# First loads and splits in a new order around a transposed x

## What is computed

```python
def hybrid_layer(x, mem, pos, g_mix, w_in, w_pa, w_pb, w_pm, w_o, g_mem, w_mkv, g_mlp, w_up, w_down):
    h = rms_norm(x, g_mix)
    z = h @ w_in
    ...
    o_m = memory_attn(q_m * scale, rms_norm(mem, g_mem), w_mkv)
    ...
    x = x + y @ w_o
```

## Time and profile before

| | |
|---|---|
| three runs | 1579.76, 1580.19, 1582.11 us; median 1580.19 |
| profiled execution | 1578.82 us, its span 1577.0 us |
| TensorE busy | 1429.0 us (91%) |
| VectorE, ScalarE, GpSimd busy | 576.1, 551.9, 674.3 us |
| DMA | 395.40 MB, mean 251 GB/s |
| mean granted clock of TensorE | 0.952 |

### The profile page before, as it was taken

The page is one execution under the profiler, slowest core; times in us unless marked ns, Lnnn a source line. Parts: engine busy times, 40 slices in busy tenths (PEclk is TensorE's granted clock), DMA queues, the critical chain, the costliest instruction groups (busy, mean ns, idle before and its releaser), DMA issues.

```text
span 1577.0 us, 17946 instructions
## 1 busy us (share of the span) xinstructions
PE 1429.0 (91%) x7601; PEld 1016.2 (64%) x7601; DVE 576.1 (37%) x885; ACT 551.9 (35%) x709; POOL 674.3 (43%) x187
## 2 busy tenths in 40 slices
PE   8999999999999999999999999999996676676666
PEld 7877788877887778887799888978841121121111
DVE  4522423336262242334643876768510010010001
ACT  6356443433535645444343344574310000000001
POOL 6846588755784658786655775010000000000000
PEclk9999999999999999999999999999998787787788
DMA  8534457588553445659925444013999999999997
GB/s 296 187 111 157 149 174 239 183 301 315 176 183 122 151 143 185 226 176 338 321 83 190 132 149 152 20 68 137 420 402 428 428 427 428 429 426 428 427 428 292
DMA packets 115517, 395.40 MB, mean 251 GB/s; under 512 B 5719, under 2 KB 9620, under 8 KB 101996
## 3 DMA queue, kind: packets, MB, share of 16 engines
q1 hardware_dynamic: 113372, 388.70, 66.0%
q0 software_dynamic: 1520, 4.49, 0.8%
q10 hardware_dynamic: 544, 1.05, 0.2%
HBM read 393.16 MB, written 1.05 MB: 250 GB/s over the span
## 4 chain that ended last, share of the span: by engine, by line
PE 75%; DMA 21%; ACT 1%; DVE 1%; issue 1%; SPq 1%; POOL 0%; DVEq 0%; ACTq 0%
PE psum L2282 17%; PE psum L2284 17%; PE psum L2283 17%; DMA ring<-in_w_e_down 7%; PE psum L1247 7%; DMA ring<-in_w_e_up 6%; DMA ring<-in_w_e_gate 6%; PE psum L1162 2%; PE psum L2435 1%; PE psum L2462 1%; PE psum L2326 1%; PE psum L1023 1%; PE psum L2511 1%; PE psum L821 1%; PE psum L823 1%; PE psum L822 1%
## 5 line engine op out<-in xcount | busy, mean ns | idle before, releaser
L655 POOL TENSOR_TENSOR ring_lo<-ring,ring_hi 128x2048 fp32r<-128x2048 f32 x118 | 538.7, 4572 | 230.2 <-ACT ring_hi L635 229.9
L635 ACT ACTIVATE ring_hi<-ring 128x2048 fp32r<-128x2048 f32 (+1 forms) x127 | 239.9, 1889 | 319.6 <-DMA ring<-in_w_down 104.2
L2284 PE MATMUL psum<-ring_hi,hT_hi 128*128 128x512 f32 (+2 forms) x848 | 327.8, 387 | 0.0
L2283 PE MATMUL psum<-ring_lo,hT_hi 128*128 128x512 f32 (+2 forms) x848 | 327.2, 386 | 0.0
L2282 PE MATMUL psum<-ring_hi,hT_lo 128*128 128x512 f32 (+2 forms) x816 | 323.2, 396 | 0.4 <-POOL ring_lo L655 0.2
L1247 PE MATMUL psum<-arena 128*32 128x512 f32 x796 | 141.9, 703 | 63.5 <-DMA arena<-in_w_e_down 23.4
L1247 PE MATMUL psum<-ring,arena 128*32 128x512 f32 x720 | 133.7, 732 | 61.2 <-DMA ring<-in_w_e_gate 23.6
L2284 PEld LDWEIGHTS psum<-ring_hi,hT_hi 128*128 128x128 f32 x848 | 159.3, 188 | 32.3
L2283 PEld LDWEIGHTS psum<-ring_lo,hT_hi 128*128 128x128 f32 x848 | 159.6, 188 | 28.8
L2282 PEld LDWEIGHTS psum<-ring_hi,hT_lo 128*128 128x128 f32 x816 | 153.5, 188 | 37.1 <-issue 6.1
L1247 PEld LDWEIGHTS psum<-arena 128*32 128x32 f32 x796 | 32.1, 126 | 163.3 <-issue 73.4
(11 more groups left out here) (467 smaller groups left out, 1927.8 us busy)
## 6 DMA issues: line engine op xcount, KB each, us to landing
ring<-in_w_in SPq DMA_DIRECT2D x59, 1024.0 KB, 5.1
ring<-in_w_up SPq DMA_DIRECT2D x32, 1024.0 KB, 5.5
ring<-in_w_down SPq DMA_DIRECT2D x32, 1024.0 KB, 5.6
ring<-in_w_e_down SPq DMA_DIRECT2D x16, 2048.0 KB, 20.5
arena<-in_w_e_up SPq DMA_DIRECT2D x14, 2048.0 KB, 20.4
arena<-in_w_e_down SPq DMA_DIRECT2D x12, 2048.0 KB, 23.8
ring<-in_w_e_gate SPq DMA_DIRECT2D x12, 2048.0 KB, 22.9
arena<-in_w_e_gate SPq DMA_DIRECT2D x12, 2048.0 KB, 22.8
```

What stands on the lines that cost most here:

```text
L635: act.activation(slot_hi(u)[:, 0:c, :], slot(u)[:, 0:c, :], ACT.Copy).then_inc(hi_sb, 1)
L655: eng.tensor_tensor(slot_lo(u)[:, 0:c, :], slot(u)[:, 0:c, :], slot_hi(u)[:, 0:c, :].bitcast(F32), ALU.subtract).then_inc(done, 1)
L2283: pe.matmul(dst, hi(k0 + k), w_lo, start=False, stop=False)
L2284: last = pe.matmul(dst, hi(k0 + k), w_hi, start=False, stop=stop and k == nk - 1)
```

## The change

Two new inputs are prepared: x transposed, `x_t` (features by tokens), and the gains of `norm_mix` as columns, `gain_cols`. The tile `xn`, not in use at that time, holds the transposed x as `xT`.

- **Loads.** ScalarE issues the first half of xT (512 features, rows of 1 KB). SyncE issues the gain columns ahead of the identity, then unit 0 in four pieces, unit 1 in two halves, the second half of xT, units 2 and 3, and the small rows, the `norm_mix` rows now among them. Token-major x is one load, which ScalarE issues when unit 2 has landed; memory and the constants go when unit 3 has landed.
- **TensorE.** The transposes of the gain rows and of both halves of x in layer 0 are gone. The identity is multiplied five times instead of four. Unit 1 is done in halves (`second_unit`).
- **ScalarE.** For each k: a block of `hT_hi` from `xT`, then a piece of unit 0. Then unit 1 in halves, the second half of `hT_hi`, the x load, units 2 and 3, the squares of x (their junk output in `x_sq` instead of `xn`), unit 4, and the wait for memory as before.
- **VectorE.** For each k a block of `hT_lo` and a piece of unit 0, then unit 1 in halves, the second half of `hT_lo`, and the low part of unit 2, which was GpSimd's.
- Counts of the semaphores follow.

```diff
-LO_VECTOR = [(l, u) for l in range(DEPTH) for u in SPLIT if (l == 0 and u < 2) or (u >= 50 and u % 4 == 2)]
+LO_VECTOR = [(l, u) for l in range(DEPTH) for u in SPLIT if (l == 0 and u < 3) or (u >= 50 and u % 4 == 2)]
...
         def _(sp):
             sp.sem_inc(slots_free, R1)
+            sp.dma_start(cols[:, 0:16], w["gain_cols"]).then_inc(const_in, 16)
             sp.dma_start(consts[:, 0:P], w["consts"][:, 0:P]).then_inc(const_in, 16)
...
-            gain_rows(0, "norm_mix", const_in)
...
+                    if l == 0 and u == 1:
+                        for half in range(2):
+                            cs = slice(2 * half, 2 * half + 2)
+                            sp.dma_start(slot(1)[:, cs, :], src[:, cs, :]).then_inc(landed(1) if half else half_in, 16)
+                        sp.dma_start(xT[:, 4:8, :], x_src[:, 4:8, :]).then_inc(rest_in, 16)
+                        continue
                     load(u, src, l * UNITS1 + u + 1)
                     if l == 0 and u == R1 - 1:
+                        gain_rows(0, "norm_mix", late_in)
...
             pe.wait_ge(const_in, 32)
-            pe.transpose(psum[:, 7, 0:16], rows1[0:16, :], ident[0:16, 0:16]).then_inc(cols_full, 1)
-            pe.wait_ge(x_in, 16)
-            half_to_features(x, 0)
-            keep_busy(6, 4)
+            keep_busy(6, 5)
             first_unit()
-            pe.wait_ge(rest_in, 16)
-            half_to_features(x, 1)
+            second_unit()
...
+            def second_unit():
+                for half in range(2):
+                    pe.wait_ge(lo_v, UC + half + 1)
+                    for t in range(TT):
+                        last = split_product(DB[1][:, t, :], tokens(hT_hi, t), tokens(hT_lo, t), 2 * half, 1, nk=2, first=2 * half,
+                                             start=half == 0, stop=False)
+                last.then_inc(slots_free, 1)
...
-            low_piece(0)
-            low_half(0, g_feat[:, 0, 0, :], 0)
-            for k in range(1, UC):
+            dve.wait_ge(const_in, 32)
+            for k in range(UC):
+                dve.wait_ge(turn_a, k + 1)
+                dve.scalar_tensor_tensor(out=hT_lo[:, k, :], in0=xT[:, k, :], scalar=g_feat[:, 0, 0, k:k + 1],
+                                         in1=hT_hi[:, k, :].bitcast(F32), op0=ALU.mult, op1=ALU.subtract).then_inc(turn_lo, 1)
                 low_piece(k)
-            split_lo(dve, 0, 1)
+            for half in range(2):
+                cs = slice(2 * half, 2 * half + 2)
+                dve.wait_ge(hi_sb, UC + half + 1)
+                dve.tensor_tensor(slot_lo(1)[:, cs, :], slot(1)[:, cs, :], slot_hi(1)[:, cs, :].bitcast(F32), ALU.subtract).then_inc(lo_v, 1)
...
-                low_half(1, g_feat[:, 0, l, :], l * 18 + 4)
+                low_half(1, g_feat[:, 0, l, :], l * 18 + 4, None if l else xT)
                 if l == 0:
-                    dve.wait_ge(cols_full, 2)
+                    split_lo(dve, 0, 2)
+                    dve.wait_ge(cols_full, 1)
...
-            x_src = w["x"].rearrange("b (t p) d -> p (b t) d", p=P)
-            act.dma_start(x[:, :, 0:UN], x_src[:, :, 0:UN]).then_inc(x_in, 16)
-            act.dma_start(x[:, :, UN:D], x_src[:, :, UN:D]).then_inc(rest_in, 16)
+            act.dma_start(xT[:, 0:4, :], w["x_t"].rearrange("(c p) t -> p c t", p=P)[:, 0:4, :]).then_inc(x_in, 16)
...
-            high_piece(0)
-            act.wait_ge(cols_sb, 1)
-            high_half(0, g_feat[:, 0, 0, :], 1)
-            for k in range(1, UC):
+            act.wait_ge(const_in, 32)
+            act.wait_ge(x_in, 16)
+            for k in range(UC):
+                act.activation(hT_hi[:, k, :], xT[:, k, :], ACT.Copy, scale=g_feat[:, 0, 0, k:k + 1]).then_inc(turn_a, 1)
                 high_piece(k)
+            for half in range(2):
+                cs = slice(2 * half, 2 * half + 2)
+                act.wait_ge(slot_in[1] if half else half_in, 16)
+                act.activation(slot_hi(1)[:, cs, :], slot(1)[:, cs, :], ACT.Copy).then_inc(hi_sb, 1)
+            high_half(1, g_feat[:, 0, 0, :], 0, xT)
+            act.wait_ge(slot_in[2], 16)
+            act.dma_start(x[:, :, :], w["x"].rearrange("b (t p) d -> p (b t) d", p=P)).then_inc(x_in, 16)
...
                 if l == 0:
-                    high_parts(1, 2)
+                    high_parts(2, 3)
+                    act.wait_ge(x_in, 32)
+                    squares_half(0, sums, x_sq)
+                    squares_half(1, sums, x_sq)
+                    high_parts(4, 4)
...
-            pool.wait_ge(rest_in, 16)
-            pool.wait_ge(slot_in[2], 16)
+            pool.wait_ge(slot_in[3], 16)
             pool.dma_start(mem_tok, w["mem"].rearrange("b (t p) d -> p (b t) d", p=P)).then_inc(mem_in, 16)
             pool.dma_start(consts[:, P:], w["consts"][:, P:]).then_inc(mem_in, 16)
```

More of the change, by code:

```diff
@@ L164 @@
 N_ROWS2 = sum(r[2] for r in ROWS2)
-N_LATE = 2 + len(ROWS2)
+N_LATE = 3 + len(ROWS2)
 PIECES = UC - 1
+EXTRA = PIECES + 1
 def rows_of(a):
@@ L286, in build @@
         mem_sq = carve(18688, TT, D)
+        x_sq = carve(16384, TT, D)
+        xT = xn[:, :, :].rearrange("p t (c n) -> p (t c) n", n=T)
         kv_mem = carve(14848, TT, 2 * WM)
@@ L2569, in _, with low_half @@
         def _(dve):
-            def low_half(half, gain, ready):
+            def low_half(half, gain, ready, features=None):
                 for k in range(4):
@@ L2574, in low_half @@
                         dve.wait_ge(turn_a, ready + k + 2)
-                    dve.scalar_tensor_tensor(out=hT_lo[:, 4 * half + k, :], in0=flat[2 + half][:, k * T:(k + 1) * T],
+                    src = flat[2 + half][:, k * T:(k + 1) * T] if features is None else features[:, 4 * half + k, :]
+                    dve.scalar_tensor_tensor(out=hT_lo[:, 4 * half + k, :], in0=src,
                                              scalar=gain[:, 4 * half + k:4 * half + k + 1],
@@ L2679, in _ @@
                 for half in range(2):
-                    dve.wait_ge(turn_full, l * 8 + 3 + half)
+                    dve.wait_ge(turn_full, l * 8 + 1 + half)
                     for k in range(4):
@@ L2888, in _, with high_half, squares_half @@
         def _(act):
[L2889 to L2890 removed]
+            def high_half(half, gain, full, features=None):
+                if features is None:
+                    act.wait_ge(turn_full, full)
+                else:
+                    act.wait_ge(rest_in, 16)
                 for k in range(4):
[L2892 removed]
+                    src = flat[2 + half][:, k * T:(k + 1) * T] if features is None else features[:, 4 * half + k, :]
+                    act.activation(hT_hi[:, 4 * half + k, :], src, ACT.Copy,
                                    scale=gain[:, 4 * half + k:4 * half + k + 1]).then_inc(turn_a, 1)
[L2895 removed]
+            def squares_half(half, into, junk=xn):
                 for t in range(TT):
[L2897 removed]
+                    act.activation(junk[:, t, half * UN:(half + 1) * UN], x[:, t, half * UN:(half + 1) * UN], ACT.Square, accum_out=into[:, t, half:half + 1])\
                        .then_inc(sq_a, 1)
[L2900 to L2902 removed]
+            act.dma_start(xT[:, 0:4, :], w["x_t"].rearrange("(c p) t -> p c t", p=P)[:, 0:4, :]).then_inc(x_in, 16)
             act.wait_ge(cleared, 1)
@@ L2990, in high_y @@
                 def high_y(half):
-                    act.wait_ge(turn_full, l * 8 + 5 + half)
+                    act.wait_ge(turn_full, l * 8 + 3 + half)
                     act.activation(hT_hi[:, 4 * half:4 * half + 4, :], flat[2 + half].rearrange("p (k t) -> p k t", k=4), ACT.Copy,
@@ L3063 @@
     arrays["consts"] = constants()[1]
+    arrays["x_t"] = np.ascontiguousarray(np.asarray(inputs["x"])[0].T)
+    arrays["gain_cols"] = np.ascontiguousarray(np.asarray(inputs["norm_mix"]).reshape(16, P).T)
     nc = bacc.Bacc("TRN2", target_bir_lowering=False, num_devices=1, dynamic_dma_scratch_size=8192)
```

48 lines of the change are left out of this document (19 added, 29 removed).

## The result

| | before | after |
|---|---|---|
| median of 21 runs each | 1580.79 us | 1582.91 us |
| ratio after / before | | 1.0018, 95% from 1.0012 to 1.0023 |
| profiled execution, its span | 1578.82, 1577.0 us | 1582.06, 1580.3 us |
| start of unit 0, 1, 2, 3 on TensorE | 9.10, 16.26, 22.17, 27.75 | 7.96, 15.06, 20.87, 26.44 |
| start of unit 4 on TensorE | 34.85 | 37.88 |

The change makes the kernel slower by 0.18%, 2.9 us, with an interval of 1.9 to 3.6 us; the difference of the two medians is 2.1 us and lies inside it. One of the 21 runs before took 2928.48 us, and the ratio leaves it out. The forecast was no change. TensorE leads by 1.1 to 1.3 us as far as unit 3 and is 3.0 us behind from unit 4 on.

What follows compares the result with a forecast made beforehand. Bound: TensorE's progress before about 1100 us, which moves the expert-weight tail. Unit 4: TensorE alone 34.85 - 2.1 = 32.8, z's tile 28.7 + 6.1 = 34.8; the later counts, so no change: 1580.2 us, range 1577.5 to 1583.2.

Steps and rivals of the forecast that it cites:

- head start: TensorE's gain from the earlier unit 0 and the dropped transposes: 2.1 us, from 1.4 to 2.6.
- memory comes late: Rival: x, unit 4 and unit 5 all pass before memory's end; M = 31, 2.3 us lost, 1582.5 us; chance 0.23.
- M: The moment when memory and the constants have all landed, as ScalarE sees it; 25.84 us before.
- What bounds the kernel: Whatever TensorE gains or loses before about 1100 us moves the expert-weight tail's start, and the end, by as much.
- Unit 0 at 7.5: TensorE starts unit 0 at 7.5 us instead of 9.10, with the first weight piece seen at 6.0.
- Units 1 to 3: These units on TensorE cost nothing; cover 1.1 us at unit 1, 0.3 at unit 2, 0.7 at unit 3.
- GpSimd's issue at 18.4: GpSimd issues memory and the constants at 18.4 us, 3.2 later than before.
- The rival of VectorE holding up the descriptors: VectorE's unit 2 subtraction delays the making of memory's load: M = 30.1, 1.4 us lost, 1581.6 us; chance 0.05.
- M = 28.7: Memory and constants landed at 28.7 us, the middle between 27.7 without unit 5 ahead and 29.6 with 0.8 MB of it.
- slack: Time before M that x and unit 4 fill, while before only POOL's load was on its way: about 0.7 us.
- cross-check: Second count of M: 25.84 + 3.2 = 29.0 if the queues looked the same from the later issue on.
- M + 6.1: z's first tile, which TensorE's unit 4 waits for, is ready 6.1 us after M, the table load setting the root.

Runs made afterwards that it cites:

- e_b_delay: The kernel before, with TensorE turning memory three times instead of once in layer 0; ratio to before 1.0018 [1.0010, 1.0027].
- e_root_vector: After, with x's root taken separately, units 4 and 5 earlier on ScalarE, unit 4's low part on VectorE, memory's mean scaled in ScalarE's root; ratio to before 0.9982.
- e_b_mem_late: The kernel before, with memory and constants asked for when unit 3 has landed instead of unit 2; ratio to before 1.0006 [0.9997, 1.0014].
- e_warm: After, with TensorE turning memory three times instead of once in layer 0; ratio to before 1.0013 [1.0005, 1.0022].
- e_late_consts: After, with the big constants issued after GpSimd's low part of unit 3 and waited for only ahead of the rotary tables; ratio to before 1.0008.
- e_early_warm: e_root_vector with constants issued once memory landed, TensorE multiplying zeros from 1.1 us and the identity ten times, unit 2 in halves; ratio to before 0.9995.

## Why the prediction was wrong

The forecast was a draw, the head start earned and given back; the measured time lies in its range, but the loss is real. What came is the rival "memory comes late", with M = 31.7 where it had put 31.

- **What bounds the kernel** held: no new wait behind unit 4, and what happened in the first 40 us reached the end. "As much" was too simple: 4.65 us at 78 us came out as 2.9 us [1.9, 3.6]. For e_b_delay (3.8 us, 2.9 [1.6, 4.3]) and from after to e_root_vector (5.5 us, 5.7) the times allow that all of it passes on.
- **Unit 0 at 7.5**: 7.96. The first piece was seen at 6.46, not 6.0: the 13 us around it moved 349 GB/s where before moved 368, so the small rows cost more than I allowed: 6.46 is 0.7 us above 7.13 - 1.4, and my upper bound was 0.5. The fast spacing began at 11.4, not 10.3. Head start 1.3 us at units 2 and 3 for a forecast of 2.1, and below the bound of 1.4. This term was wrong too, but M covered it: the later of the two counts is the chain's.
- **Units 1 to 3**: right. Unit 2 was ready at 20.52, TensorE came at 20.5; VectorE needed 2.29 in one piece where I counted 2.5. No wait. The two just meet, so 0.3 us of cover was all used.
- **GpSimd's issue at 18.4**: 18.80, right. The rival of VectorE holding up the descriptors has no evidence for it: q0's first packets came 3.5 us after the issue, before 3.3 (15.20 to 18.5).
- **M = 28.7: this is the step that failed.** "At 412 GB/s a further 1.05 MB is 2.55 us. It is less by the slack ... about 0.7 us", and for unit 5 half of 1.9 us. Neither size was right. Some slack was there and was filled (0.80 MB from 16 to 19 us before, 0.99 after), but as much was lost earlier, where the loads have smaller rows (4.79 MB from 2 to 15 us before, 4.53 after). On balance the added bytes passed at 379 GB/s, so 1.05 MB is 2.8 us. And 1.17 MB more of q1's weights went in between, 3.1 us, where I allowed 0.4 MB. The two make up the 5.9 us by which M moved, because 379 GB/s is taken from them; that M moves by about half a us between profiles of the same loads limits this split as well. The cross-check (M "3.2 later than before" because the issue is) rested on M following its issue; e_b_mem_late shows that it does not, 3.1 us of issue made 0.4 us of M.
- The reason behind the second size: I read the near-empty q1 at 23 to 24 us as a queue that doesn't cut in. Unit 5's load had been issued only at 22.00, and its packets came in numbers from 25 us on, 3 us later, as x's, which took 3.8, and GpSimd's, which took 3.3 and 3.5. It had hardly begun. In after it was issued 1.3 us earlier and memory's load began 3.8 us later, so from 24 us on both moved at once, and q1 took 0.09 to 0.36 MB of every microsecond from 24 to 31. The Trainium skill (DMA: Bandwidth & Descriptors, Queues, rings and completion order) says that each DMA engine takes turns between the queues for which it has work, a packet at a time. The trace agrees where both have work: 66 packets against 67 from 21 to 22 us before; towards the end of the constants it is 39 against 80. By that rule unit 5 would have been counted as passing beside memory for as long as memory took, which is the late rival.
- **M + 6.1**: right. 31.70 to the end of z's first tile at 37.83 (36.42 + 1.41, as long as before) is 6.1 us, and the table load set the root (34.11 + 1.28 = 35.39, root at 35.41). VectorE's operation took 1.14, to the end of GpSimd's subtraction at 35.31 (30.76 + 4.55).
- **Not foreseen at all**: the low clock behind the gap, 1.6 us (e_warm). I priced a wait at its own length. And a loss of 0.18% could be told from no change, where I had put the limit at 0.2%.
- A second limit was missed too: x holds ScalarE until 29.30 even without the constants (e_late_consts), so with M at 28.7 memory's squares would still have begun 0.6 us later than I said.

The sum with the measured terms: 34.85 - 1.3 (head start kept) = 33.55 for TensorE alone; z's tile at 31.7 + 6.1 = 37.8; the later counts, 37.8, plus 1.6 of low clock: 4.6 at the q/k mark, measured 4.65.

## What to carry to other kernels

A load that is moved twice isn't hidden by queues that are full: count every byte that passes before the landing you care about, the next loads on the other queues too, at the rate of that stretch, and check whether the consumer needs one of them or all. Price a gap on TensorE at its length plus the slow matmuls behind it, here 1.6 to 2.7 us behind gaps of 3.4 to 4.6. A head start is worth what the longest chain behind it lets through: here the root of x shared an instruction with memory's. Taking it apart brought 0.18% slower back to no change, and with unit 4's low part on VectorE and memory's mean out of the way of z's tiles it was 0.18% faster.

## What the runs showed of the hardware

- A load asked for while the queues are full starts late: x was issued at 15.80 and q10 had no packet until 19.6, and GpSimd's load at 18.80 none until after 22. Before, GpSimd's took 3.3 us, while q1 was at work. With no other load on the queues, a unit issued at 40.60 before had its first packets between 41.5 and 42.
- VectorE's small operation from SBUF to SBUF took 0.17 us with GpSimd at rest, and 0.72 (e_warm), 1.14, 1.96, 2.28, 2.60 and 4.75 beside its subtractions, ending each time within 0.05 us of the end of one of them. The 4.75 is the odd one: it began 0.1 us before the second of three subtractions ended and wasn't let in between the second and the third.
- At the start of unit 0 the matmuls stand 0.43 us apart for 3.4 us while the granted clock of that stretch reads 1.00; behind the wait at unit 4 the same spacing goes with a reading of 0.61. In e_early_warm, where TensorE worked from 1.13 us on, unit 0 stands 0.23 us apart from its second matmul on. So the slow start goes with the idle time ahead of it, and the reading of 1.00 in these first microseconds doesn't show it; the spacing does.
